# Streaming encoder step: modulation and first column tiles in eight pieces of two contraction tiles instead of four blocks of four

## The reference, cut to what matters

```python
shift, scale, gate = split(silu(c) @ w_ada + b_ada)     # one c for the prompt, one for the sample
h = x * (1 + scale) + shift
z = h @ w_in                                            # 5192 columns: qa ka va ga qb kb vb gb qi ki wi
...                                                     # two attention groups
y = concat(oa * silu(ga), ob * silu(gb)) @ w_out
out = LayerNorm(ALPHA * x + gate * y)
```

## Time and profile before

| | |
|---|---|
| time, median of 3 runs | 2037.24 us (2036.79 to 2039.54) |
| profiled execution, its own time | 2037.48 us |
| profiled execution, span | 2035.8 us |
| PE busy | 1901.1 us, 93% of the span |
| first stage: first modulation product | 14.75 us |
| first unit of block 0, 1, 2, 3 | 61.59, 117.01, 172.53, 228.15 us |
| end of the last unit | 259.6 us |

### The profile page before, as it was taken

How to read it: one execution, slowest core, us unless ns; L and a number is a source line. 1 busy time by engine, 2 the same in 40 slices (tenths; PEclk the granted TensorE clock), 3 DMA queues, 4 the chain that set the end, 5 groups by cost and what they waited for, 6 DMA issues and landing times.

```text
span 2035.8 us, 36028 instructions
## 1 busy us (share of the span) xinstructions
PE 1901.1 (93%) x13207; PEld 1575.7 (77%) x13207; DVE 952.6 (47%) x2480; ACT 624.2 (31%) x1349; POOL 679.5 (33%) x850
## 2 busy tenths in 40 slices
PE   3999999999999999999999998989998899999992
PEld 0766787769999999999999996656665677778672
DVE  0333403467777788873000006977775022232726
ACT  0121233321111111111111117978886211112120
POOL 0122211012222222222222225866665434344741
PEclk7888899979999999999999999999998999999996
DMA  8666233112222322222222235431210333336463
GB/s 265 198 215 211 77 101 114 32 31 85 87 85 84 94 85 89 84 84 84 89 84 84 84 113 128 107 81 40 56 45 18 111 104 109 114 116 178 122 210 90
DMA packets 198321, 213.23 MB, mean 105 GB/s; under 512 B 22128, under 2 KB 145520, under 8 KB 197376
## 3 DMA queue, kind: packets, MB, share of 16 engines
q1 hardware_dynamic: 177648, 177.16, 30.6%
q10 hardware_dynamic: 19232, 30.30, 4.0%
q0 software_dynamic: 1328, 4.26, 0.7%
HBM read 181.31 MB, written 34.55 MB: 106 GB/s over the span
## 4 chain that ended last, share of the span: by engine, by line
issue 44%; PE 26%; POOL 17%; ACT 5%; DVE 4%; DMA 2%; POOLq 1%; SPq 0%; ACTq 0%; DVEq 0%
POOL w_lo L988 8%; POOL w_lo L1037 8%; PE psum L1538 4%; PE psum L1495 3%; PE psum L1517 3%; PE psum L1376 2%; PE psum L1378 2%; PE psum L1377 2%; ACT p_rows L883 2%; PE psum L1404 2%; PE psum L1336 2%; PE psum L1406 1%; PE psum L1405 1%; DMA ada_ring<-in_w_ada_dram 1%; PE psum L1359 1%
## 5 line engine op out<-in xcount | busy, mean ns | idle before, releaser
L1404 PE MATMUL psum<-h_hi,w_hi 128*128 128x364 f32 (+1 forms) x1728 | 577.9, 334 | 7.6 <-POOL w_lo L988 6.9
L1406 PE MATMUL psum<-h_lo,w_hi 128*128 128x364 f32 (+1 forms) x1728 | 567.7, 329 | 0.0
L1405 PE MATMUL psum<-h_hi,w_lo 128*128 128x364 f32 (+1 forms) x1728 | 566.0, 328 | 0.0
L988 POOL TENSOR_TENSOR w_lo<-w_raw,w_hi 128x512 fp32r<-128x512 f32 x144 | 185.3, 1287 | 708.3 <-ACT w_hi L742 708.0
L1404 PEld LDWEIGHTS psum<-h_hi,w_hi 128*128 128x128 f32 x1728 | 326.0, 189 | 45.4 <-issue 36.8
L1405 PEld LDWEIGHTS psum<-h_hi,w_lo 128*128 128x128 f32 x1728 | 326.1, 189 | 0.0
L1406 PEld LDWEIGHTS psum<-h_lo,w_hi 128*128 128x128 f32 x1728 | 325.7, 188 | 0.0
L1037 POOL TENSOR_TENSOR w_lo<-w_raw,w_hi 128x512 fp32r<-128x512 f32 x128 | 184.1, 1439 | 220.8 <-ACT w_hi L928 220.8
L742 ACT ACTIVATE w_hi<-w_raw 128x512 fp32r<-128x512 f32 x144 | 90.7, 631 | 480.7 <-PE psum L1406 453.9
L1580 PE MATMUL psum<-w_hi,h_hi 128*128 128x512 f32 x576 | 227.5, 395 | 10.7 <-POOL w_lo L1037 10.7
L1581 PE MATMUL psum<-w_lo,h_hi 128*128 128x512 f32 x576 | 225.8, 392 | 0.0
(11 more groups left out here) (208 smaller groups left out, 2604.5 us busy)
## 6 DMA issues: line engine op xcount, KB each, us to landing
w_raw<-in_w_in_dram SPq DMA_DIRECT2D x160, 256.0 KB, 2.8
ada_ring<-in_w_ada_dram SPq DMA_DIRECT2D x64, 512.0 KB, 5.0
w_raw<-in_w_out_dram SPq DMA_DIRECT2D x256, 128.0 KB, 2.9
z_transposed<-z_evacuated ACTq DMA_DIRECT2D x32, 544.0 KB, 2.7
stage<-in_w_ada_dram SPq DMA_DIRECT2D x32, 512.0 KB, 4.0
over_z_evacuated<-z_transposed SPq DMA_DIRECT2D x32, 272.0 KB, 4.3
x_block<-in_x_prompt_dram SPq DMA_DIRECT2D x4, 2048.0 KB, 8.5
q_transposed<-z_transposed SPq DMA_DIRECT2D x16, 272.0 KB, 5.0
```

The costliest lines, as they stand in the source:

```text
L988: pool.tensor_tensor(v(wlo), raw3[ch][:, :, 0:width], v(whi).bitcast(F32), ALU.subtract).then_inc(lo_ready.sem, 1)
L1404: pe.matmul(Z, w(whi), hh[:, kt_, a:b], start=(kt_ == 0), stop=False)
L1405: pe.matmul(Z, w(wlo), hh[:, kt_, a:b], start=False, stop=False)
L1406: ins = pe.matmul(Z, w(whi), hl[:, kt_, a:b], start=False, stop=(kt_ == KT - 1))
```

## The change

The width is gone through in eight pieces `p` of two contraction tiles (`PIECE_KT = [2] * 8`) instead of four blocks of four.

- An `ada_step` multiplies four runs of 128 columns instead of four of 256; there are 8 x 16 of them instead of 4 x 16. A ring slot still has 512 KB but holds two contraction tiles of half as many columns: two loads of 256 KB (rows of 1 KB instead of 2 KB) fill it, and it is freed after two steps.
- A unit has 2 x 3 = 6 matmuls instead of 12; there are 120 units instead of 60, so DVE empties twice as many banks. A column tile's weights are 256 columns wide in SBUF instead of 512, and there are 40 of them.
- The preparation of piece p + 1 is spread among the units of piece p. Modulation steps 6 to 15 follow units 0, 0, 1, 2, 3, 4, 4, 5, 6, 7; DVE copies the rows (one copy, all partitions) after unit 7; `columns(p + 1)` (one product instead of eight) follows unit 9; a third of the turning of `x` (`turn_x`) follows each of the units 10, 11 and 12, with ACT's, DVE's and POOL's part in the same places of their lists; steps 0 to 5 of piece p + 2 follow units 9 to 14. The first six steps of piece 1 stand between the turns of piece 0.
- The modulation uses banks 6 and 7 in turn; `mod` has two buffers; the banks are set to zero once at the start, so that the copy of all partitions reads only numbers.
- SP's list is rewritten: for each piece its eight slots, with `load_x` after slot 4 and a `load_first` after slots 1, 3, 4, 5 and 7.

```diff
+PIECE_KT = [2] * 8
+NP = len(PIECE_KT)
+ADA_SLOTS = [4 * nk for nk in PIECE_KT]
+A_EARLY, A_UNITS, MOD_UNIT, X_UNIT = 6, 8, 9, 10
...
+def step_unit(s):
+    return (s - A_EARLY) * A_UNITS // (KT - A_EARLY)
...
     @block.sync
-        def load_ada(j, k):
-            n = j * KT + k
+        def load_ada(p, i):
+            n, c0, nk = ADA_AT[p] + i, P * KT0[p], PIECE_KT[p]
             sp.wait_ge(ada_used.sem, ada_used.at(n + 1 - ADA))
...
+                for s in range(2):
+                    sp.dma_start(ada_slot(p, i)[:, :, s], w_ada[:, k0:k0 + ks, s, c0:c0 + P * nk]).then_inc(ada_loaded[n % ADA].sem, 16)
...
         def load_first(n):
...
+            sp.wait_ge(first_lo.sem, first_lo.at(n + 1 - RAW))
...
-        for j in range(3):
-            for k in range(KT):
-                if k == 3:
-                    load_x(j + 1)
-                load_ada(j + 1, k)
-                if k % 3 == 0 and k < 15:
-                    load_first(NF * j + RAW + k // 3)
+        for p in range(1, NP):
+            e = ADA_SLOTS[p] // 8
+            for i in range(ADA_SLOTS[p]):
+                load_ada(p, i)
+                if i == 4 * e:
+                    load_x(p)
+                if i == e and p > 1:
+                    load_first(NF * (p - 1) + 3)
+                if i in (3 * e, 4 * e, 5 * e, 7 * e):
+                    load_first(NF * (p - 1) + 4 + (3 * e, 4 * e, 5 * e, 7 * e).index(i))
...
     @block.gpsimd
+        for p in range(NP):
+            for f in range(2, 5):
+                lo_first(NF * p + f)
+            if p + 1 < NP:
+                for slot in range(3):
+                    low_rows(x_units(p + 1, slot))
+                    if slot == 1:
+                        lo_first(NF * p + 5)
+                lo_first(NF * p + 6)
...
     @block.tensor
-        for j in range(4):
-            columns(j)
-            for f in range(NF):
-                for c in range(len(TCH)):
-                    first_unit(j, f, c)
-                    if j < 3:
-                        ada_step(j + 1, f * len(TCH) + c)
-            if j < 3:
-                ada_step(j + 1, KT - 1)
+        columns(0)
+        for i, u in enumerate(range(3 * KT0[0], 3 * KT0[1])):
+            turn_x(u)
+            if i < A_EARLY:
+                ada_step(1, i)
+        for p in range(NP):
+            for u in range(UNITS):
+                first_unit(p, u)
+                if p + 1 < NP and u == MOD_UNIT:
+                    columns(p + 1)
+                if p + 1 < NP and X_UNIT <= u < X_UNIT + 3:
+                    for x in x_units(p + 1, u - X_UNIT):
+                        turn_x(x)
+                if p + 1 < NP:
+                    for s in range(A_EARLY, KT):
+                        if step_unit(s) == u:
+                            ada_step(p + 1, s)
+                if p + 2 < NP and 0 <= u - MOD_UNIT < A_EARLY:
+                    ada_step(p + 2, u - MOD_UNIT)
```

More of the change, by code:

```diff
@@ L52, with x_units, piece_of, ada_landed @@
 RAW, SPLIT = 4, 2
+PIECE_KT = [2] * 8
+NP = len(PIECE_KT)
+KT0 = [sum(PIECE_KT[:p]) for p in range(NP + 1)]
+ADA_SLOTS = [4 * nk for nk in PIECE_KT]
+ADA_AT = [sum(ADA_SLOTS[:p]) for p in range(NP + 1)]
+N1 = NF * NP
+A_EARLY, A_UNITS, MOD_UNIT, X_UNIT = 6, 8, 9, 10
+def step_unit(s):
+    return (s - A_EARLY) * A_UNITS // (KT - A_EARLY)
+def x_units(p, slot):
+    nk = PIECE_KT[p]
+    return [3 * KT0[p] + nk * slot + i for i in range(nk)]
+def piece_of(kt_):
+    return max(p for p in range(NP) if KT0[p] <= kt_)
+def ada_landed(n):
+    return sum(32 if KT0[p + 1] - KT0[p] == 2 else 16 for p in range(NP) for i in range(ADA_AT[p], ADA_AT[p + 1]) if i <= n and (n - i) % ADA == 0)
+def last_first(slots, s):
+    return max(n for n in range(N1) if n % slots == s)
 Y_GROUPS = [[0, 1, 2, 3, NTILE - 1], [4, 5, 6, 7]]
@@ L291, in build @@
     raw_loaded = [count(f"raw_loaded{s}") for s in range(RAW)]
+    first_loaded = [count(f"first_loaded{s}") for s in range(RAW)]
+    first_hi = count("first_hi")
+    first_lo = count("first_lo", RAW)
+    rows_zeroed = count("rows_zeroed")
     lo_ready = count("lo_ready", RAW)
@@ L587, in load_w @@
+        for n in range(NF * (NP - 1) + 3, N1):
+            load_first(n)
         def load_w(m, ch, col, width):
-            sp.wait_ge(lo_ready.sem, lo_ready.at(m * WCH + (ch + 1 - RAW)))
+            sp.wait_ge(lo_ready.sem, lo_ready.at(m * WCH + (ch + 1 - RAW - NF * WCH)))
             sp.dma_start(raw3[ch][:, :, 0:width], w_in[:, WCH * ch:WCH * ch + WCH, ds(col, width)])\
@@ L720, in _ @@
         hi_first(0)
         hi_first(1)
-        for j in range(4):
[L723 to L731, removed]
+        for slot in range(3):
+            for u in x_units(0, slot):
+                modulate(u)
@@ L1362, in first_unit, with ada_step @@
-        def first_unit(j, f, c):
-            n, v = j * NF + f, j * UNITS + f * len(TCH) + c
+        def ada_step(p, k):
+            per = KT // ADA_SLOTS[p]
+            i, nk = k // per, PIECE_KT[p]
+            n = ADA_AT[p] + i
+            if k == 0 and p > 1:
+                pe.wait_ge(mod_row.sem, mod_row.at(p - 1))
+                pe.wait_ge(mod_ready.sem, mod_ready.at(p - 1))
+            pe.wait_ge(ada_loaded[n % ADA].sem, ada_loaded[n % ADA].at(ada_landed(n)))
+            for t in range(4):
+                ins = pe.matmul(bank(6 + p % 2)[32 * t:32 * t + 2, 0:64 * nk], cTv[:, k, :],
+                                ada_slot(p, i)[:, k % per, t // 2, 64 * nk * (t % 2):64 * nk * (t % 2 + 1)],
+                                start=(k == 0), stop=(k == KT - 1), tile_position=(0, 32 * t))
+            if k % per == per - 1:
+                ins.then_inc(ada_used.sem, 1)
@@ new lines, in columns, with turn_x @@
+        def columns(p):
+            pe.wait_ge(mod_row.sem, mod_row.at(p + 1))
+            for h in range(PIECE_KT[p] // 2):
+                ins = pe.matmul(bank(6 + p % 2)[:, 256 + 8 * h:264 + 8 * h].rearrange("p (i w) -> p i w", w=2), modrow[:, P * h:P * h + P],
+                                ident[:, :].rearrange("p (i c) -> p i c", c=32)[:, :, 0:2], start=True, stop=True)
+            ins.then_inc(mod_psT.sem, 1)
+        def turn_x(u):
+            kt_, (lo, hi) = u // 3, XCH[u % 3]
+            p = piece_of(kt_)
+            if u == 3 * KT0[p]:
+                pe.wait_ge(x_loaded.sem, x_loaded.at(32 * p + 32))
+            if u >= 2:
+                pe.wait_ge(hf_ready.sem, hf_ready.at(u - 1))
+            at = P * (kt_ % 4)
+            for t in range(lo // P, (hi + P - 1) // P):
+                r = tile_rows(t)
+                ins = pe.transpose(bank(4 + u % 2)[:, P * t - lo:P * t - lo + r], xb[0:r, t, at:at + P], ident[0:r, 0:r])
+            ins.then_inc(xT_ready.sem, 1)
```

242 lines of the change are left out of this document (130 added, 112 removed).

## The result

The changed kernel took 2049.04 us (median of six, 2037.31 to 2056.82); the kernel before, in turns with it on the same chip, 2037.01 (six, 2030.23 to 2039.54). The ratio is 1.0065, 95% interval 1.0041 to 1.0089: **slower by 0.65%**. The forecast was 2029 and faster; the time lies 2 us above the range.

A forecast was written before the change was run, and what follows sets the result against it. First stage bound by weight waits, then preparation, then busy PE; first unit 37.4, piece 0 25.5 + 3.0 + 2, then 142.5, 24.8, 15.3, clock 1: end 251.5 against 259.6, 8 us less, 2029 us; range 2014 to 2047.

The forecast's parts named there:

- Start: Up to the first unit: smaller first loads and preparation bring it to 37.4 instead of 61.59, 24 us gained.
- PE's work for a piece: Units, steps, transitions, turns and columns of a middle piece: 25.5 us, against 27.7 for half a block before.
- What SP is blocked by: SP's list in each piece: load_first holds ring slots back, so a piece waits 3.0 us (bounds 0.5 and 7).
- slot 6's 2.3: PE behind units 3 and 4: slot 6 lands 5.7 us after unit 2, wanted after 3.35, a wait of 2.3 us.
- DVE's narrow place: Behind units 10 to 12 DVE ends the last low half 1 us before unit 0 wants it: 0.5 us a piece.
- The clock: First stage: 2 us while the clock rises in piece 0, and 1 us for its falling in one wait.
- Carried over one to one: Behind the first stage: kernel runs as before, so the stage's end, 251.5 against 259.6, gives 2029.4 from 2037.5.
- the transitions added per block: PE's units and steps: twice as many units and step places cost 3 us more transitions per block.
- the 2.1 us ahead of slot 6's load: From unit 2's end through ACT, POOL and SP's issue of the tile: 2.1 us before 3.6 of landing.
- The first: Rival, ring loads: land as today, 5.0 rather than 3.6 us; waits 7 us a piece, 2055, slower; chance 0.14.
- The second: Rival, thirds or waits: clock falls in every piece, 2.5 to 3.5 us each, 2050, slower; chance 0.11.
- The break-even of 4.2 us a piece: First stage: 4.2 us of waiting per piece over seven pieces puts the end where the kernel was.

The follow-up runs named there:

- reordered list: Changed kernel with SP's list in the order its waits end (x after slot 2, each tile one or two slots later): 2002.05 us, ratio 0.9835; again 2004.02.
- ring loaded once: Changed kernel with modulation-weight loads after the first three slots left out, steps multiplying those three over and over: 1990.67 us, ratio 0.9774 to before.
- x late, tiles in order: Changed kernel with tiles in the order their waits end, but x's loads left behind slot 4: 2040.14 us, ratio 1.0023 to before.
- The control: The changed kernel run once more, unchanged: 2044.81 us, ratio 1.0051 to the kernel before.
- x earlier: Changed kernel with only the loads of x moved, from behind slot 4 to behind slot 2: 2032.10 us, ratio 0.9995 to before.
- the two half edits: Against the changed kernel: only x moved behind slot 2 (2032.10 us), or only tiles put in order of their waits, x behind slot 4 (2040.14 us).
- one tile moved: Changed kernel with the tile ahead of slot 6 moved behind slot 7 in SP's list: 2047.23 us, ratio 1.0054 to before.

## Why the prediction was wrong

The mechanism was right: SP's list holds loads back and PE waits for them behind unit 3 or 4 of each piece. Two terms of the sum were too small, and together they turned its sign: the time that slot 5's loads need behind x, and what the clock costs behind a wait. The stage ends at 267.2 instead of 251.5. Of these 15.7 us the waits for the ring are 6.5 (27.0 in all for 20.5), the clock 9.6 (10.6 for 1; that is what is left of pieces 1 to 6 behind PE's own time, 25.01 and 23.14, and the waits). The other terms nearly cancel. With the waits alone the stage would have ended at 258.0, still ahead of before; with the clock alone at 261.1. Term by term:

- *Start*: first unit 37.07 for 37.4, by luck. The first modulation ended at 29.7 for 27.9, and the preparation behind it took 7.4 for 9.4, so that two errors of some 2 us cancel. The last two steps of the first modulation:

```profile
28.65 1.03 PE L1443 MATMUL psum<-ada_ring,c_transposed 128*2 128x128 f32 x16 [1.64 <-DMA ada_ring<-in_w_ada_dram]
```

- *PE's work for a piece*: 25.01 (reordered list, ring loaded once) for 25.5. Right. A step, a run of eight, takes 0.40, and turns follow each other every 0.11 (forecast 0.4 and 0.11). In piece 6 the six missing early steps save 25.01 - 23.14 = 1.9, not 3.2: 0.31 each, which makes that piece 0.9 longer than worked out. Piece 7 took 15.97 for 15.3.
- *What SP is blocked by*: that `load_first` would stand in the list and hold slots back was right, the size wasn't: the first failing step. The row came out as 28 times and 120 us, four tiles a piece, for "seven times some 4 us". For slot 5 the prediction had x's 1.1 MB "with 1.2 MB around them", 7 us at 330 GB/s, and a wait no larger than slot 6's 2.3. In piece 3 slot 5 landed 9.8 us after x's issue (129.52 to 139.32), in which 2.8 MB moved at 290 GB/s: slower, and half a MB more, since the loads issued behind slot 5 (from 135.35 on) share the rate before it has landed. The wait is 3.85 there, and 3.9 in the mean of seven pieces, for a forecast of 3.0 that held 0.5 for DVE's narrow place; a wait for DVE shows only at the first units of pieces 0 and 7 (2.2 together). The tile ahead of slot 4, where SP stands until 128.08 while DMA is at 0.39, adds to it, but little: with that tile out of the way (x late, tiles in order) the wait is still 3.1 in the mean.
- *The clock*: the second failing step, and the larger. The forecast was 1 us in the whole stage. In pieces 0 to 5 PE was busy 26.6 to 27.3 us for the same work as 25.0 at full clock, 1.6 to 2.3 us more in each, at a mean clock of 0.94 (piece 2: 0.89). Waits and clock together make pieces 1 to 5 longer than forecast by 11.7 us (154.15 for 142.5), piece 6 by 4.5.
- *Carried over one to one*: 2029.4 + 15.7 gives 2045.1. The control measured 2044.8, the first comparison 2049.0. No trace is of an execution of 2049; the stretch up to the end of the logits, whose length differs by 6 us from one execution of the changed kernel to the next (165.3 and 171.3), can hold the difference.

Slips in the working that change nothing: the tile ahead of slot 4 is 5q + 4, the transitions added per block are nearer 4 us than 3 by its own 0.32, and the named parts of the 2.1 us ahead of slot 6's load add up to 1.8.

Of the rivals, two are half right. The first asked for a landing of 5.0 us. The median at L606 from the first unit on is 3.9:

```profile
L606 SPq DMA_DIRECT2D ada_ring<-in_w_ada_dram x104: 367/470/1624, 35.8 to 230.2; - x104
...
DMA to landing us min/median/max: 2.8/3.9/7.7
```

But the loads that decide, slot 5's, took 6.5 and 6.8. The second, a fall of the clock in every piece, came true at 1.6 to 2.3 us each for its 2.5 to 3.5, though not by the turns: with the same 18 turns among the units the reordered list keeps 1.00 in its pieces, and in the changed kernel the clock falls behind the wait for the ring. The rule of the Trainium skill behind that rival ("TensorE: Matmul & The Clock Gate", Part 4: PE-mode transpose: transposes don't count as busy like matmuls) may hold for a stretch of turns alone, as in the preparation of before; with units between the turns, no run here shows a cost. The break-even of 4.2 us a piece was worked out with waits alone; with 1.8 us of clock behind each wait, as in the changed kernel, it lies near 2.4, below the wait that I forecast. Where the clock fell in only four of seven pieces (x earlier), 2.9 us of waiting a piece still left the stage's end 1.9 ahead of before. So the forecast's own waits lay close to break-even, and the clock behind them should have been priced.

What slot 5 waited for is shown by removing it (x earlier: the wait moves to slot 6 and 2.4 in the mean) and by removing both (no wait). That x, as against the tiles, would do without the other is refuted by the two half edits. That slot 5 lands so late behind x is told by the times of one queue: in piece 3 its first load, issued 1.8 us after x's, landed 1.7 behind it (137.80 to 136.07). The Trainium skill ("DMA: Bandwidth & Descriptors", Two DMAs through the same engine are not ordered) says that descriptors of one queue of a DMA engine start in order but overlap. The trace agrees with both: in the run with one tile moved the first load of slot 5 in piece 3 landed at 139.99, ahead of the sample's rows of x, issued 1.3 us before it (140.24).

## What to carry to other kernels

An in-order list of loads is part of the schedule: when work is cut finer, sort the list by the time at which each load's place comes free, and look for every load that stands behind one with a later condition or behind a large transfer, since the waits on SP (`load_first` 120 us) tell it at a glance. Waits for loads that follow one another in one list hide each other, so that removing one uncovers the next and most of the gain comes only with the last (9, 9 and 37 us here). Where PE waits for some us, add what the clock can cost behind the wait (1.6 to 2.3 us a piece here).

## What was not expected of the hardware

- SP's own time for issuing a load isn't constant: 0.37 to 0.65 us at L557 before, up to 1.62 at L606 after. Of the eighteen over 0.7 us seventeen start within 9 us behind a load of x: the two loads of slot 5 took 2.10 together at 131.29, two of the same size at 128.50 0.98. What SP then waits for, no run separates.
- The length of a wait alone doesn't say whether the clock falls behind it: with x earlier it fell behind waits of 2.25 and 2.4 us and not behind one of 2.8.
- The clock near the end of the logits (400 to 435 us) is at 0.50 in some executions of a kernel and near 1.00 in others, and moves the rest of the program by some 6 us. The runs show that the change doesn't decide it; what does stays open.
